# Turning C's probabilities on TensorE in one of four stages, bias rows fetched per layer, and B's keys ahead of C's last low rows

## The reference

```python
h = einsum('bsd,de->bse', x, w_in)          # columns: A, B and C parts with their gates
a_out = pool_mixer(a_v, a_group_w, a_scale) * silu(a_gate)
b_out = swa_sink_attention(b_q, b_k, b_v, b_sinks) * silu(b_gate)
c_out = chunk_relbias_attention(c_q, c_k, c_v, c_rel_bias) * silu(c_gate)
y = einsum('bse,ed->bsd', concat([a_out, b_out, c_out]), w_out)
x = layer_norm(ALPHA * x + y, ln_gain, ln_bias)

# C: each chunk of 64 rows sees itself and the 8 chunks before it
s = einsum('bnqhd,bnkhd->bnhqk', qc, kb) * (C_HEAD_DIM ** -0.5)
s = where(valid, s + rel_bias[:, clip(t - s)], NEG_INF)
o = einsum('bnhqk,bnkhd->bnqhd', softmax(s), vb)
```

## Time and profile before

| | us |
|---|---|
| median of 3 runs | 2868.71 (2867.33 to 2870.06) |
| the profiled execution | 2868.0 |
| its span, first to last instruction | 2866.2 |
| TensorE busy | 2784.3 |
| VectorE / ScalarE / GpSimd busy | 1827.2 / 1265.9 / 1294.8 |
| granted TensorE clock, mean | 0.989 |
| C stages, it = 0 to 3 | 0 to 364.5, 711.5 to 1106, 1453.1 to 1792.4, 2139.5 to 2507.1 |
| B and output stages | 347.0, 347.1, 347.1, 347.6 long |

### The profile page before, as it was taken

One profiled execution on the slowest core, in us unless ns is written; L12 is line 12 of the kernel. 1 busy time (PEld: TensorE's weight loads), 2 busy tenths in 40 slices (PEclk: granted clock), 3 DMA queues, 4 the chain that ended last, 5 costly groups with the idle time before them and its releaser, 6 DMA issues.

```text
span 2866.2 us, 41006 instructions
## 1 busy us (share of the span) xinstructions
PE 2784.3 (97%) x12836; PEld 2315.2 (81%) x12836; DVE 1827.2 (64%) x2950; ACT 1265.9 (44%) x2612; POOL 1294.8 (45%) x927
## 2 busy tenths in 40 slices
PE   7999999999999998999999999999999999899998
PEld 6888888888787777888888887888888888788886
DVE  4666678722677767883257776796236787678624
ACT  3444466523344435653234444565234444466521
POOL 3444454444444344444454444444444444444441
PEclk9999999999999999999999999999999999999999
DMA  5555533355777863225567775323557777532442
GB/s 174 159 170 164 154 101 87 92 178 176 207 207 219 216 174 96 85 84 169 168 190 198 210 206 161 102 84 102 176 177 215 208 214 212 141 99 81 130 160 103
DMA packets 470981, 448.04 MB, mean 156 GB/s; under 512 B 257664, under 2 KB 308896, under 8 KB 467104
## 3 DMA queue, kind: packets, MB, share of 16 engines
q1 hardware_dynamic: 467024, 430.19, 52.1%
q10 hardware_dynamic: 3792, 15.73, 1.4%
HBM read 358.69 MB, written 90.27 MB: 157 GB/s over the span
## 4 chain that ended last, share of the span: by engine, by line
PE 78%; DVE 8%; DMA 6%; issue 3%; SPq 3%; ACT 1%; POOL 0%; ACTq 0%; POOLq 0%; DVEq 0%
PE acc L706 52%; PE sc L706 16%; PE pv L706 9%; DMA pt_raw<-c_prob_scratch 2%; DMA raw<-in_wall 2%; DVE pt L1526 1%; SPq L517 1%; PE sc L775 1%; DVE res L1694 1%; DMA bias_rows_scratch<-bias_row_scratch 1%; DVE mixh L1526 1%; DMA c_prob_scratch<-prob 1%; SPq L480 1%; DVE mixl L1526 1%; DVE res L1691 1%
## 5 line engine op out<-in xcount | busy, mean ns | idle before, releaser
L1494 POOL TENSOR_TENSOR wl<-raw,wh 128x512 fp32r<-128x512 f32 x920 | 1294.0, 1412 | 1528.1 <-ACT wh L1052 1519.1
L1052 ACT ACTIVATE wh<-raw 128x512 fp32r<-128x512 f32 x920 | 573.7, 629 | 1136.5 <-PE acc L706 693.7
L706 PE MATMUL acc<-xh,wh 128*128 128x512 f32 x2560 | 1010.6, 395 | 20.8 <-POOL wl L1494 17.2
L706 PE MATMUL acc<-xl,wh 128*128 128x512 f32 x2560 | 1002.2, 391 | 0.0
L706 PE MATMUL acc<-xh,wl 128*128 128x512 f32 x2560 | 1001.4, 391 | 0.0
L706 PEld LDWEIGHTS acc<-xh,wh 128*128 128x128 f32 x2560 | 484.2, 189 | 119.3 <-issue 20.9
L706 PEld LDWEIGHTS acc<-xh,wl 128*128 128x128 f32 x2560 | 483.5, 189 | 104.2
L706 PEld LDWEIGHTS acc<-xl,wh 128*128 128x128 f32 x2560 | 484.1, 189 | 92.7
L1526 DVE TENSOR_TENSOR xl<-prob,xh 128x512 f32 x48 | 55.7, 1160 | 237.6 <-ACT xh L1052 237.6
L706 PE MATMUL sc<-wh,mixh 128*128 128x512 f32 x496 | 193.5, 390 | 0.1
L706 PE MATMUL sc<-wl,mixh 128*128 128x512 f32 x496 | 193.0, 389 | 0.0
(11 more groups left out here) (221 smaller groups left out, 3678.4 us busy)
## 6 DMA issues: line engine op xcount, KB each, us to landing
raw<-in_wall SPq DMA_DIRECT2D x920, 256.0 KB, 2.8
c_prob_scratch<-prob SPq DMA_DIRECT2D x128, 160.0 KB, 3.0
pt_raw<-c_prob_scratch SPq DMA_DIRECT2D x32, 640.0 KB, 5.2
res_scratch<-res ACTq DMA_DIRECT2D x12, 1024.0 KB, 4.1
res<-res_scratch SPq DMA_DIRECT2D x12, 1024.0 KB, 5.1
res<-in_x SPq DMA_DIRECT2D x8, 1024.0 KB, 6.9
x_scratch<-res SPq DMA_DIRECT2D x8, 1024.0 KB, 5.2
x_t_scratch<-turned SPq DMA_DIRECT2D x128, 64.0 KB, 2.5
```

The source lines that it names most:

```text
L706: return nc.tensor.matmul(o, lhsT, rhs, start=start, stop=stop)
L1052: return nc.scalar.activation(o, i, ACT.Copy, scale=scale)
L1494: nc.gpsimd.tensor_tensor(wl[:, s, :], raw[:, s, :], wh[:, s, :].bitcast(F32), ALU.subtract).then_inc(w_lo, 1)
```

## The change

In the second half of the first layer (`on_tensor(it)`, it = 1) a new pair routine turns the probabilities on TensorE: `c_transpose` runs five transposes of 128x128 for each head from `prob` back into `sc[h]`, ACT's `c_hi` and DVE's `c_lo` read them from there, and all four steps are attended within their own pair. DVE's block transpose, the stores and the load of the scratch are gone there. In the other three stages they stay. Then: `bias_rows` handles one layer, for the first layer in the same four places (the second one later), for the second layer during it = 1, and pair 0 waits for its own semaphore `tz_first`; at a C stage's end `b_keys_hi` and `b_query` stand ahead of C's last low rows or product; the cosines and sines are loaded a little earlier; in the first halves `centre` stands behind `c_lo(3)`; in it = 3 the order on ACT and DVE at a pair's start is another.

```diff
-ROPE_AT = (C_PAIRS * 24 + 11, C_PAIRS * 24 + 12)
+ROPE_AT = (C_PAIRS * 24 + 11, C_PAIRS * 24 + 8)
...
+        def on_tensor(it):
+
+            return it == 1
...
+        def c_out(it, j):
+            if j == 3 and on_tensor(it):
+                return sc[0][:, 0:512]
+            return pv[:, 512 * (j % 2):512 * (j % 2) + 512]
...
-                            sp.wait_ge(tz_out, max(p, 1) * (16 * DEPTH) + 16 * DEPTH)
+                        if it == 0:
+                            sp.wait_ge(tz_out if p else tz_first, max(16 * p, 16))
+                        if it == 2 and p == 0:
+                            sp.wait_ge(tz_second, 16 * C_PAIRS)
...
                 for h in range(2):
-                    if c_step(it, p, j):
+                    if on_tensor(it):
+                        pe.wait_ge(ct_turned_lo, 2 * c_kind(it, p, j) + h + 1)
+                    elif c_step(it, p, j):
                         pe.wait_ge(cs_exp, 2 * c_step(it, p, j) + h - 1)
...
+            def c_transpose(it, p, j):
+                for h in range(2):
+
+                    pe.wait_ge(cs_scaled, 2 * c_kind(it, p, j) + h + 1)
+                    for b in range(5):
+                        cs = slice(b * P, (b + 1) * P)
+                        last = nc.tensor.transpose(sc[h][:, cs], prob[:, h, cs], ident[:])
+                    last.then_inc(ct_full, 1)
...
+                    c_scores(it, p, 0)
+                    quarter(17, 0)
+                    quarter(18, 0, part=range(0, 2))
+                    c_transpose(it, p, 0)
+                    quarter(18, 0, part=range(2, 4))
+                    c_scores(it, p, 1)
...
+                    c_attend(it, p, 0)
+                    quarter(19, 0)
+                    quarter(20, 1, part=range(0, 1))
+                    c_transpose(it, p, 1)
+                    quarter(20, 1, part=range(1, 4))
+                    c_scores(it, p, 2)
+                    c_attend(it, p, 1)
+                    quarter(21, 1)
+                    quarter(22, 1, part=range(0, 1))
+                    c_transpose(it, p, 2)
...
+                    quarter(22, 1, part=range(1, 4))
+                    c_scores(it, p, 3)
+                    c_attend(it, p, 2)
+                    quarter(23, 1)
+                    c_transpose(it, p, 3)
+                    pe.wait_ge(prod_ok, p * 2 + (MIXES * it + 3))
+                    quarter(24, 0)
+                    c_attend(it, p, 3)
...
+                    slot(17)
+                    c_exp(it, p, 0)
+                    slot(18)
+                    c_hi(it, p, 0)
+                    slot(19)
+                    c_exp(it, p, 1)
+                    slot(20)
+                    c_hi(it, p, 1)
...
                     if p:
                         c_add(it, p - 1, 2)
                     turn_values(p)
-                    if it:
-                        centre(it - 1, p)
                     mixed_low(p)
                     if p:
                         c_lo(it, p - 1, 3)
+                    if it:
+                        centre(it - 1, p)
...
                 def second_half(p):
                     if p:
+                        c_max(it, p - 1, 3)
                         c_lo(it, p - 1, 1)
-                        c_max(it, p - 1, 3)
+                        gate_ready(p * 2 + MIXES * it, 1)
+                        c_add(it, p - 1, 0)
                     coefficients(p)
...
-                c_add(it, p, 2)
+                if not on_tensor(it):
+                    c_add(it, p, 2)
                 rotated_query(ROTS * it + 1, 0)
+                if half(it) and not on_tensor(it):
+                    c_lo(it, p, 3)
                 rotate(it, 1, KV0 + 7, 1, 1.0)
-                c_lo(it, p, 3)
+                if not half(it):
+                    c_lo(it, p, 3)
```

More of the change, by code:

```diff
@@ L397, in c_step, with c_kind @@
             return (it * C_PAIRS + p) * 4 + j
+        def c_kind(it, p, j):
+            return (sum(on_tensor(i) == on_tensor(it) for i in range(it)) * C_PAIRS + p) * 4 + j
         def c_seen(it, j):
@@ L589, in pair_events @@
                         store_ln(it - 1, p)
-                    if s in (21, 22) and turns(it) and not half(it):
+                    if s in (21, 22) and turns(it):
                         store_turned(it - 1, p, s - 21)
@@ L603, in pair_end @@
                     if it:
[L604 to L607, removed]
+                        if turns(it):
                             store_turned(it - 1, p, 3)
@@ L614, in _ @@
                         pair_events(p, s)
[L615 to L622, removed]
-                                store_turned(it - 1, q, t)
-                    if u == ROPE_AT[half(it)]:
+                    if u == ROPE_AT[on_tensor(it)]:
                         sp.wait_ge(cs_max, 8 * C_PAIRS * (it + 1))
@@ L627, in _ @@
                         sp.dma_start(brope[:, 1, :], rope_sin[half(it)]).then_inc(rope_in, 16)
+                    for q in range(C_PAIRS):
+                        for j in range(4):
+                            if not on_tensor(it) and u == q * U_C + STORE_AT[half(it)][j]:
+                                store_c_prob(it, q, j)
+                            if not on_tensor(it) and u == q * U_C + LOAD_AT[half(it)][j]:
+                                load_c_prob(it, q, j)
                     load_unit(it, u, u % RING, u if u < B0 else B0 + (u - B0 + 4) % U_B)
@@ L1259, in pair @@
                     slot(16)
+                    if first:
+                        bias_rows(0, 1, tz_out)
                     slot(17)
@@ L1515, in _ @@
             dv.sem_inc(c_fold, 2)
+            dv.sem_inc(ct_turned_lo, 2)
             dv.sem_inc(bt_lo, 4)
@@ L1916, in _ @@
                     c_add(it, p, 1)
-                else:
+                elif not half(it):
                     c_max(it, p, 3)
```

306 lines of the change are left out of this document (243 added, 63 removed).

## The result

The changed kernel takes 2820.1 us (median of 4, 2819.6 to 2820.7), the kernel before 2868.0 in the same runs: a ratio of 0.983 (95% interval 0.982 to 0.985), 1.7% faster. Forecast were 2819.

What follows compares the result with a forecast made beforehand. TensorE, busy 2784.3 of 2866.2 us, was taken as the bound, so only its idle time and half clock could go. 18 + 16 + 4.5 + 3.5 + 8 + 0 = 50 off 2868.7 gave 2819 us, range 2804 to 2848.

Steps and rivals of the forecast that it cites:

- Turning, the price: it = 1: 160 added transposes on TensorE at 0.11 us each, 17.6 us, all on the engine that sets the end.
- Turning, the waits: it = 1: 6 us of waits taken; the stage becomes 376 us, 18 us shorter, bounds 24 shorter to 16 longer.
- it lacks 0.4 in the first step: it = 1: a pair's first step has 7.7 us of TensorE time for a chain of 8.1 us.
- DVE is full, 9.0 of 8.9: it = 1: DVE's work in a step is 9.0 us of the 8.9 available, which leaves no cushion.
- rival 1: it = 1: chain doesn't fit as DVE is full, steps wait 1.5 us; 2853 at worst, 2845 middle; chance 0.15.
- Rival 2: it = 1: ACT's splits still wait for weights, now inside the chain, 52 us more than taken, 2871; chance 0.04.
- the base of 352.5: C stages of it = 1 and it = 3: some 352.5 us is what a second half costs when nothing waits.
- Bias rows: it = 0: one DMA issue instead of four removes two TensorE stops and half clock, 16 us, between 8 and 18.
- Ends of the stages: C stage ends, reordered on ACT and DVE: 4 to 5 us in it = 0, 3.5 in it = 2, 8 in it = 3.
- Keys, query and product still follow one another on ACT and DVE: End of it = 3: reason that a third of the 11.3 us at stake may stay; 8 us taken, 2 to 12.
- The gate behind `c_lo(1)`: it = 3: gate_ready(1) now stands behind c_lo(1), some 0.7 us before TensorE wants it: 0, up to -3 us.
- The moved `centre`: it = 2: attend waits of 2.8 us go, but the next step's scores wait instead: nil, from -5 to +3 us.

Runs made afterwards that it cites:

- experiment 8: Changed kernel with a second scaling by 1.0 of each head's probabilities on VectorE in every step of it = 1: 2824.6 us, ratio 0.985.
- experiment 4: Kernel before with only the bias rows and the ends of the C stages changed, no transposes on TensorE, no moved centre: 2853.1 us, ratio 0.995.
- experiment 1: Kernel before with the bias rows alone changed, the second layer's sent during it = 1: 2862.3 us, ratio 0.998.
- experiment 2: Kernel before with the bias rows alone changed, the second layer's sent in it = 0 instead of it = 1: 2856.4 us, ratio 0.996.
- experiment 5: Changed kernel with centre in the first halves moved back ahead of the low parts: 2813.9 us, ratio 0.981.
- experiments 5 to 8: Changed kernel with, in turn, centre moved back, turning also in it = 3, every transpose twice, a second scaling in it = 1: 2813.9, 2821.5, 2837.9, 2824.6 us.

## Why the prediction was right, and where it was not

**Turning, the price: right.** 160 transposes at 0.11 us were taken, 0.105 measured by doubling. The earlier trace rows gave the right price because it shows four of them between two matmuls whose spacing is known; the duration in the row (0.27) overlaps with the next. The Trainium skill's figure (TensorE: Matmul & The Clock Gate, Part 4), about 275 ns in a kernel, is that duration and not what a row of them costs; and its remark that transposes don't count for the clock gate changed nothing here, the granted clock was 1.00 with 320 of them.

**Turning, the waits: too many taken.** I took 6 us for it = 1, and there are none. The working was right in its sizes: a chain of 8.1 us was forecast for a step and is 8.2 (828.07 to 836.3), TensorE's own time 8.9 and is 9.1, so the 0.8 to spare is 0.9. What was wrong is "it lacks 0.4 in the first step": TensorE's time there is 7.76 us (820.31 to 828.07), as forecast, but the chain is 7.5 (head 0's low part is ready near 827.85), not 8.1. So 0.2 is spare, and the changed kernel doesn't wait. "DVE is full, 9.0 of 8.9" was wrong too: in the second step it stands nearly 2 us, and in experiment 8 at least 1.0 us more a step cost only 7.3 in 16 steps instead of 16 or more. I had put the folds and a gate into every step, and the scaling at 0.63, which without the block layout takes 0.55. With this rival 1 falls. Nor did the working ask why it = 1 lost so much more than it = 3; the turned layer norm rows between stores and load (experiment 4) were not in it. Rival 2 (ACT's splits late for weights) fell as well: with no stop of TensorE in the stage, no split can have been late. Of the other 3 us of the 9, 0.8 are in the transposes and 2.1 in the base of 352.5: 367.2 - 16.8 = 350.4 is what a second half costs without waits. I had counted the half clock behind the five long stops only and not behind the small ones; the loss in it = 1 was 46.0, not 41.0.

**Bias rows: right in place, wrong in account.** 16 us were forecast for it = 0 and 17.7 came. What did not hold without the turning is that the second layer's DMAs "move into it = 1, where they have 80 us" and are "small beside 640 KB": their landing had time, but the loads that were issued just behind them had not. Without the turning they cost 12.9 us (experiments 1 and 2). It did no harm to the forecast only because the turning takes away the very loads that they delay.

**Ends of the stages: mechanism right.** In it = 0 and 2 the removed stops are worth what was said (4.1 and 3.8; 4 to 5 and 3.5 forecast), but in it = 0 the changed kernel gives it back through an attend whose low part is queued behind the rotation. I named what is late next as the query; it was this low part, one place earlier. In it = 3 3.6 of 8 us came, counting the half clock behind. "Keys, query and product still follow one another on ACT and DVE" was the point, under-priced: DVE's queue there is without a gap for 11 us, and B's values are turned last in it. The gate behind `c_lo(1)` cost 1.4, within the 0 to 3 allowed.

**The moved `centre`: the mechanism was named, the value was wrong.** Nil was taken from a range of -5 to +3; it is -5 to -6, at the edge of it. The words that DVE "now waits about 2 us for ACT's copies before it" had the loss in them: `centre` (3.87 us) had filled that wait, which is 1.8 us (0.71 and 1.08), and DVE has no gap behind it in which to make it up. The keys' low parts are ready 116.1 us into the stage (1524.15) and 113.7 us in experiment 5, 2.4 earlier, while the waits that the move relieved stood at 1 us each.

**The total** was met because these errors cancel, which is luck: 9 too little for it = 1, 3 too much for it = 0, 4.5 each for it = 2 and it = 3.

## What to carry to other kernels

An edit can be paid for by another one: the bias DMAs alone were nearly worthless and are free only since the scratch path beside them is gone, so a change of several parts wants each part run alone and in pairs before it is given a price. Where a load is late, look first at what stands before it in the queue that issues it: here moving what stood there is an edit that adds no work, and it was not tried alone. Turn data on TensorE where the trip through memory costs more than 0.11 us a tile in waits, and not where it costs less: in it = 3, which does the same matmuls, it did not pay. Before moving a long operation, look at the queue behind it up to the next deadline and at the wait that it filled, not only at the wait that it relieves.

## What the runs showed of the hardware

- A DMA of 384 KB in 256 rows on ACT's queue doubled the time of a 640 KB load issued on SP's queue 1.2 us later (8.59 us against 4.2), in experiment 1; without it, other loads of that size took 4.2 to 8.6 us in the same stage. In experiment 2 the last of four stores beside such a DMA took 9.7 to 10.3 us to land in three pairs, against 2.5 to 2.7 in experiment 1.
- Additions of VectorE with all operands in SBUF can stand while GpSimd works: two that take 0.29 us each in the median took 2.75, ending with GpSimd's two operations (319.95 to 322.70 and 319.94 to 322.56), while an operation of VectorE that reads PSUM (324.11, 0.69 us) ran at its usual time. That agrees with the Trainium skill (SBUF — State Buffer, SBUF: two separate sides): the two engines share a pair of ports under an exclusive lock, which an operation of VectorE with two SBUF inputs also needs against one of GpSimd that reads SBUF. In the six profiles with the same code at the end of it = 0 (the changed kernel twice, experiments 5 to 8) VectorE's operations there were longer than usual by 3.2, 3.2, 3.2, 2.2, 2.2 and 1.3 us in all, and TensorE stood 2.7, 1.9, 1.9, 0.6, 0.6 and 0 us at the attend. The added scaling of experiment 8 took 0.49 us, and 1.43 to 1.44 in the four cases in which GpSimd had started just before (821.47 and 821.84).
- A stop of 3.5 us just ahead of a stage is paid a second time in it: 1.6 us of half clock over its first 17 us, which no wait in that stage shows.
